# Two transformer-like blocks on one core: the last round of the second FFN up-projection as block products, and its weight sums made on the side

## The reference

```python
x = x + gate_m * (jnp.concatenate([attn, rec], axis=-1) @ w_out[l])    # output projection, 1024 x 1024
h = rms_norm_2(x, ffn_norm_g[l]) * (1 + scale_f) + shift_f
u, v = jnp.split(h @ w_up[l], 2, axis=-1)                              # 1024 x (2816 + 2816)
u = causal_depthwise_conv(u, conv_w[l], conv_b[l])                     # 3 taps
x = x + gate_f * ((jax.nn.silu(u) * v) @ w_down[l])                    # 2816 x 1024
return rms_norm_2(x, final_norm_g)
```

## Time and profile before

| | |
|---|---|
| median of 3 runs | 1339.14 us (1339.03 to 1342.26) |
| the profiled execution: its own time | 1340.83 us |
| the profiled execution: its span, first to last instruction | 1339.0 us |
| PE busy | 1325.6 us (99%), 8520 matmuls |
| PEld busy | 1143.1 us (85%) |
| DVE / ACT / POOL busy | 874.9 (65%) / 643.3 (48%) / 682.4 (51%) us |
| mean granted TensorE clock | 0.997 |
| HBM read / written | 185.55 / 33.55 MB |

### The profile page before, as it was taken

One profiled execution on the slowest core, in us unless ns is written; L12 is line 12 of the kernel. 1 busy time (PEld: TensorE's weight loads), 2 busy tenths in 40 slices (PEclk: granted clock), 3 DMA queues, 4 the chain that ended last, 5 costly groups with the idle time before them and its releaser, 6 DMA issues.

```text
span 1339.0 us, 22719 instructions
## 1 busy us (share of the span) xinstructions
PE 1325.6 (99%) x8520; PEld 1143.1 (85%) x8520; DVE 874.9 (65%) x1711; ACT 643.3 (48%) x1146; POOL 682.4 (51%) x378
## 2 busy tenths in 40 slices
PE   8999999999999999999999999999999999999998
PEld 7878888888998888888889986778998999998887
DVE  5898976455778676767897878823479655541222
ACT  7336566464255444444222535585364666642222
POOL 7577444326354444444553489743355555554441
PEclk9999999999999999999999999999999999999999
DMA  6985696865525444444673241265335457452221
GB/s 216 226 266 203 193 154 110 121 101 170 176 80 177 153 141 141 141 147 142 204 232 124 64 126 34 64 119 87 95 134 166 134 172 213 143 208 91 87 87 63
DMA packets 251210, 191.00 MB, mean 143 GB/s; under 512 B 23001, under 2 KB 245443, under 8 KB 250608
## 3 DMA queue, kind: packets, MB, share of 16 engines
q1 hardware_dynamic: 216896, 159.79, 39.1%
q0 software_dynamic: 33024, 29.61, 12.1%
q10 hardware_dynamic: 1200, 0.36, 0.1%
HBM read 185.55 MB, written 33.55 MB: 164 GB/s over the span
## 4 chain that ended last, share of the span: by engine, by line
PE 95%; DVE 3%; ACT 1%; DMA 1%; issue 0%; SPq 0%; DVEq 0%; ACTq 0%
PE ps L2744 28%; PE ps L2745 28%; PE ps L2746 28%; PE ps L2938 2%; PE ps L2994 1%; PE ps L3023 1%; DVE qd L2394 1%; DVE hf L2402 1%; PE ps L3226 1%; DMA x_in<-in_x 1%; PE ps L3270 0%; PE ps L3255 0%; PE ps L3199 0%; DVE hs L2437 0%; PE ps L3292 0%
## 5 line engine op out<-in xcount | busy, mean ns | idle before, releaser
L973 POOL TENSOR_TENSOR w_lo<-raw,w_hi 128x1024 fp32r<-128x1024 f32 (+2 forms) x196 | 457.1, 2337 | 514.6 <-ACT w_hi L1108 381.2
L2744 PE MATMUL ps<-h_hi,w_hi 128*128 128x512 f32 (+1 forms) x1280 | 459.3, 359 | 0.0
L2745 PE MATMUL ps<-h_lo,w_hi 128*128 128x512 f32 (+1 forms) x1280 | 454.9, 355 | 0.0
L2746 PE MATMUL ps<-h_hi,w_lo 128*128 128x512 f32 (+1 forms) x1280 | 454.8, 355 | 0.0
L2744 PEld LDWEIGHTS ps<-h_hi,w_hi 128*128 128x128 f32 x1280 | 243.0, 190 | 37.7 <-issue 4.9
L2746 PEld LDWEIGHTS ps<-h_hi,w_lo 128*128 128x128 f32 x1280 | 242.7, 190 | 34.4
L2745 PEld LDWEIGHTS ps<-h_lo,w_hi 128*128 128x128 f32 x1280 | 243.1, 190 | 31.9
L1108 ACT ACTIVATE w_hi<-raw 128x1024 fp32r<-128x1024 f32 (+2 forms) x152 | 150.1, 990 | 240.6 <-PE ps L2746 215.3
L2744 PE MATMUL ps<-g_hi,w_hi 128*128 128x512 f32 (+1 forms) x394 | 145.0, 368 | 0.0
L2745 PE MATMUL ps<-g_lo,w_hi 128*128 128x512 f32 (+1 forms) x394 | 144.5, 367 | 0.0
L2746 PE MATMUL ps<-g_hi,w_lo 128*128 128x512 f32 (+1 forms) x394 | 144.5, 367 | 0.0
(11 more groups left out here) (413 smaller groups left out, 2163.3 us busy)
## 6 DMA issues: line engine op xcount, KB each, us to landing
ada<-in_ada_w SPq DMA_DIRECT2D x48, 512.0 KB, 3.8
raw<-in_ffn_w_up SPq DMA_DIRECT2D x22, 1024.0 KB, 4.9
raw<-in_w_in SPq DMA_DIRECT2D x21, 1024.0 KB, 5.3
kept_sums<-in_w_up POOLq DMA_DIRECT2D x12, 1792.0 KB, 11.9
raw<-in_w_up SPq DMA_DIRECT2D x8, 1024.0 KB, 5.0
kept_sums<-kept_sums POOLq DMA_DIRECT2D x4, 1792.0 KB, 15.8
raw<-in_ffn_w_down SPq DMA_DIRECT2D x8, 896.0 KB, 6.1
sums<-kept_sums SPq DMA_DIRECT2D x28, 256.0 KB, 5.5
```

Source lines behind the costliest of these rows:

```text
L973: pool.tensor_tensor(w_lo[w_slot(slot)][:, 0:nk, :], part[:, :, slot % 2 * P:(slot % 2 + 1) * P], w_hi[w_slot(slot)][:, 0:nk, :].bitcast(F ...
L2744: pe.matmul(out_ap, w, x, start=first, stop=False, **kw)
L2745: pe.matmul(out_ap, w, xl, start=False, stop=False, **kw)
L2746: return pe.matmul(out_ap, wl, x, start=False, stop=last, **kw)
```

## The change

- `R1` becomes 11: the rounds 3 to 10 are block products, in 16 pairs instead of 14, and the plain round 10 goes. Its four entries in the orders of ACT, DVE and PE go with it.
- The sums of weights for round 10 are made apart from those of the seven rounds before. POOL issues four copies of 512 KB, both kinds at once (`begin_sum(n, None)`), after `lo(S_OUT2 + 3)`, once all eight earlier adding transfers have landed. It then issues two adding transfers of 512 KB after `lo(S_OUT2 + 5)`, once the four copies have landed, a third after `lo(S_OUT2 + 7)`, once these two have landed, and the fourth after `lo(S_UP2 + 1)`, once the third has. SP waits for all 16 adding transfers and copies in question before it loads the first pair.
- The sets of PSUM banks are swapped: even pairs take banks 0 to 3, and the last plain round (tiles 164 to 167) takes banks 4 to 7. The two matmuls of L3323 and L3324 go.
- The last pair's first product on DVE (`gated_up(10, 0)`) waits for both results of the pair, because the low part of the fourth activation sum lies where its output goes.
- `kept_sums` has 8 rounds to a row instead of 7, so the adding transfers from one sum to the other walk rows of 7 x 128 instead of one flat run.

```diff
-R0, R1 = 3, FT // 2 - 1
+R0, R1 = 3, FT // 2
...
-            bank[s] = s % 4 + (4 if AFTER <= s < S_DOWN2 else 0)
+            bank[s] = s % 4 + (4 if PAIR_TILE - 4 <= s < PAIR_TILE else 0)
...
         def kept_blocks(kind, t, kh):
 
+            w = a["w_up_2"][0][kh * 4 * P:(kh + 1) * 4 * P, :]
+            if kind is None:
+                c = up_columns(R1 - 1, 0) + t * P
+                return w.rearrange("k (c f) -> k c f", c=2)[:, :, c:c + P]
             c = up_columns(R0, kind)
-            w = a["w_up_2"][0][kh * 4 * P:(kh + 1) * 4 * P, c:c + (R1 - R0) * 256]
-            return w.rearrange("k (r t n) -> k r t n", t=2, n=P)[:, :, t, :]
-
-        PAIR_SET = lambda p: 4 * ((p + 1) % 2)
+            return w[:, c:c + (R1 - 1 - R0) * 256].rearrange("k (r t n) -> k r t n", t=2, n=P)[:, :, t, :]
+
+        def kept_at(n, kind):
+
+            if kind is None:
+                return kept_sums[n - 1].rearrange("c k r n -> k c r n")[:, :, R1 - 1 - R0, :]
+            return kept_sums[n - 1][kind, :, 0:R1 - 1 - R0, :]
+
+        PAIR_SET = lambda p: 4 * (p % 2)
...
-            sp.wait_ge(sums_kept, SUMS_BEGUN + 16 * 8)
+            sp.wait_ge(sums_kept, SUMS_BEGUN + 16 * 16)
...
             def add_to_sum(n, kind):
...
+                pool.wait_ge(sums_kept, SUMS_BEGUN + 16 * ADDED_BEFORE[n, kind])
+                more = {1: lambda: kept_blocks(kind, 1, 1), 2: lambda: kept_at(1, kind),
+                        3: lambda: kept_blocks(kind, 1, 0), 4: lambda: kept_at(2, kind)}[n]()
+                pool.dma_start(kept_at(n, kind), more, accum_op=ALU.add, max_dma_last_dim=4 * P).then_inc(sums_kept, 16)
...
+            ADDED_BEFORE = {(1, 0): 0, (1, 1): 0, (3, 0): 0, (3, 1): 0, (2, 0): 4, (2, 1): 4, (4, 0): 6, (4, 1): 6,
+                            (1, None): 12, (3, None): 12, (2, None): 14, (4, None): 15}
...
+                         S_OUT2 + 5: [(1, None), (3, None)], S_OUT2 + 7: [(2, None)], S_UP2 + 1: [(4, None)]}
 
             def kept(s):
-                if s in ADD_STEPS:
-                    add_to_sum(*ADD_STEPS[s])
+                if s == S_OUT2 + 3:
+                    pool.wait_ge(sums_kept, SUMS_BEGUN + 16 * 8)
+                    for n in (1, 2, 3, 4):
+                        begin_sum(n, None)
+                for step in ADD_STEPS.get(s, ()):
+                    add_to_sum(*step)
...
-            for j in range(4):
-                hi(S_DOWN2 + j)
-                if j < 2:
-                    first_tap(R1, j)
-                else:
-                    silu(R1, j - 2)
-            for t in range(2):
-                g_high(R1, t)
...
-                dve.wait_ge(tile_done, up_tile(r, 1, t) + 1)
+                dve.wait_ge(tile_done, up_tile(r, 1, t) + (1 if r + 1 < R1 else 2 - t))
...
-            for t in range(2):
-                taps2(R1, t)
-            for t in range(2):
-                gated_up(R1, t)
-            for t in range(2):
-                g_low(R1, t)
...
-                if s == PAIR_TILE - 1:
-                    pe.wait_ge(lo_done, lows(s))
-                    pe.matmul(ps[5][:, 0:HALF], w_hi[s % 4][:, 0, :], h_hi[:, 0, 0:HALF], start=True, stop=True)
-                    pe.matmul(ps[6][:, HALF:T], w_hi[s % 4][:, 0, :], h_hi[:, 0, 0:HALF], start=True, stop=True)
                 tile(s, h_hi, h_lo)
...
-            pe.wait_ge(freed["dve"], after_pair(NPAIR - 1))
```

More of the change, by code:

```diff
@@ L337, in build @@
         t_at = [(ada_at, ada_at + 4096), (x_at, x_at + 4096), (x_at + 8192, x_at + 12288),
-                (G0 + 4 * T * 2 * R1, G0 + 4 * T * (FT + 2 * R1))]
+                (G0 + 4 * T * (FT - 2), G0 + 4 * T * (2 * FT - 2))]
         t_hi = [sb(f"t{n + 1}_hi", [P, 4, HALF], F32R, at=t_at[n][0])[:, :, :] for n in range(4)]
@@ L821, in hgrn_pool @@
                 lo(s)
+                kept(s)
         def add_late_squares(pool, b):
@@ L983, in begin_sum @@
                 t, kh = {1: (1, 0), 2: (0, 0), 3: (0, 0), 4: (0, 1)}[n]
-                pool.dma_start(kept_sums[n - 1][kind], kept_blocks(kind, t, kh)).then_inc(sums_kept, 16)
+                pool.dma_start(kept_at(n, kind), kept_blocks(kind, t, kh)).then_inc(sums_kept, 16)
             def add_to_sum(n, kind):
-                if n == 1:
-                    pool.wait_ge(sums_kept, SUMS_BEGUN)
-                elif n in (2, 4):
-                    pool.wait_ge(sums_kept, SUMS_BEGUN + 16 * (4 if n == 2 else 6))
@@ L992, in add_to_sum @@
-                more = {1: lambda: kept_blocks(kind, 1, 1), 2: lambda: kept_sums[0][kind],
-                        3: lambda: kept_blocks(kind, 1, 0), 4: lambda: kept_sums[1][kind]}[n]()
-                pool.dma_start(kept_sums[n - 1][kind], more, accum_op=ALU.add, max_dma_last_dim=4 * P).then_inc(sums_kept, 16)
-            SUM_STEPS = dict(zip([*range(S_V, S_MERGE), S_MERGE + 3, S_MERGE + 4], itertools.product((1, 2, 3, 4), range(2))))
-            ADD_STEPS = dict(zip([S_MERGE + n for n in (6, 8, 11, 13, 15)] + [S_ATTN + 2, S_OUT2 - 2, S_OUT2],
-                                 itertools.product((1, 3, 2, 4), range(2))))
@@ L1000, in kept @@
-            def kept(s):
-                if s in ADD_STEPS:
-                    add_to_sum(*ADD_STEPS[s])
+                pool.wait_ge(sums_kept, SUMS_BEGUN + 16 * ADDED_BEFORE[n, kind])
+                more = {1: lambda: kept_blocks(kind, 1, 1), 2: lambda: kept_at(1, kind),
+                        3: lambda: kept_blocks(kind, 1, 0), 4: lambda: kept_at(2, kind)}[n]()
+                pool.dma_start(kept_at(n, kind), more, accum_op=ALU.add, max_dma_last_dim=4 * P).then_inc(sums_kept, 16)
+            SUM_STEPS = {s: [step] for s, step in zip([*range(S_V, S_MERGE), S_MERGE + 3, S_MERGE + 4],
+                                                      itertools.product((1, 2, 3, 4), range(2)))}
@@ new lines, in _ @@
+            ADDED_BEFORE = {(1, 0): 0, (1, 1): 0, (3, 0): 0, (3, 1): 0, (2, 0): 4, (2, 1): 4, (4, 0): 6, (4, 1): 6,
+                            (1, None): 12, (3, None): 12, (2, None): 14, (4, None): 15}
+            ADD_STEPS = {S_MERGE + 6: [(1, 0)], S_MERGE + 8: [(1, 1)], S_MERGE + 11: [(3, 0)], S_MERGE + 13: [(3, 1)],
+                         S_MERGE + 15: [(2, 0)], S_ATTN + 2: [(2, 1)], S_OUT2 - 2: [(4, 0)], S_OUT2: [(4, 1)],
+                         S_OUT2 + 5: [(1, None), (3, None)], S_OUT2 + 7: [(2, None)], S_UP2 + 1: [(4, None)]}
@@ L1059, in _ @@
                     pool.wait_ge(low_or_gated, LOW_BEHIND[s])
-                if s in SUM_STEPS:
-                    begin_sum(*SUM_STEPS[s])
+                for step in SUM_STEPS.get(s, ()):
+                    begin_sum(*step)
                 kept(s)
```

## The result

| | before | after |
|---|---|---|
| median, us | 1341.76 (1339.03 to 1346.47, 20 runs) | 1347.39 (1342.62 to 1356.26, 20 runs) |
| profiled span and own time, us | 1339.0 and 1340.83 | 1343.7 and 1345.4 |
| granted clock | 0.997 | 0.997 |

The ratio is 1.0045, 95% interval 1.0033 to 1.0057: the kernel is slower by 4.4 to 7.6 us where 1.9 us less was forecast. The forecast in microseconds leaned on three runs of before at 1339.14; over 20 runs that kernel is at 1341.76, so 2.6 us of the distance to the forecast is the base and the rest the change.

The account below looks back on a forecast made before the run. PE, with 95% of the chain that ended last, was taken to bound the kernel. Savings of 1.63 and 0.23 us, 1.86 together with nothing added, took the median from 1339.14 to 1337.3 us, range 1336.5 to 1341.

Parts of the forecast that it names:

- PE's sum: Round 10 as two pairs instead of plain saves PE 1.63 us, the two dropped matmuls of L3323 and L3324 0.23 us.
- The border to the down-projection: Down-projection directly after pair 15: its first tile, banks and residual load come in time; cost taken as nothing.
- The copies: Four small copies on POOL behind tile 151: 1.02 us each to issue, landed at 949 to 956, taken as 952.5.
- Two adding issues later, at 955.2, tile 154 is subtracted ... hidden, with 3 us left: POOL in the output projection: after the copies and two adding issues, tile 154 ready at 957.6, PE wants it at 960.66.
- the late copies: Rival: the small copies land late for tile 154 in the output projection; result 1338.5 to 1343 us, chance 0.10.
- the slow chain: Rival: landing does not shrink with size, POOL waits for the third transfer, PE stands 11.7 us; 1349 to 1351, chance 0.07.
- The fourth issue: Last small adding issue on POOL, ahead of tile 158 and the squares: 1.09 us from a line over rows, cost nothing.
- the prediction's own cover of 1.42 us: Slack around the fourth issue before PE takes the squares' sum: 0.84 us ahead of tile 158 plus 0.58 us.
- the rival: The fourth issue is as long as a large one, PE stands 1.2 to 2.2 us: 1338.5 to 1339.5, chance 0.14.
- small issues over 1.4 us: Stated sign of being wrong: any of the small issues on POOL takes over 1.4 us.
- a wait of POOL for the third transfer past 977: Stated sign of being wrong: POOL waits longer than 977 for the third small adding transfer to land.
- The strided rows of the large transfers: Two large adding transfers in the output projection's lead may take 3.61 instead of 2.64 us to issue; cost taken as nothing.

Follow-up runs that it names:

- pairs only: Changed kernel without small transfers, flat rows for the large ones, last two pairs taking the sums of the pairs before them: 1339.69 us, ratio 0.999 to before.
- the three comparisons of times: Strided against flat rows: with adding transfers moved alike (ratios 0.0023 apart), in the changed kernel (0.0019), and in the kernel before (0.0010).
- ten flat profiles: Profiles of the kernels whose large transfers keep flat rows, the kernel before among them; in the others round 10's sums have a tensor of their own, `kept_last`.
- four strided ones: Profiles with eight-round rows: the changed kernel, it with adding transfers moved (1342.13 us), with only the fourth moved (1344.78), and the kernel before with that layout (1343.41).
- A copy behind the adding transfer: Changed kernel with flat rows and the fourth small copy issued behind the first small adding transfer: 1343.32 us, one run.
- Halved adding transfers: Changed kernel with flat rows and the first two small adding transfers issued in two halves each: 1345.25 us, one run.
- Placed: Changed kernel with flat rows, first small adding transfer alone, second and third sum's two products later, fourth behind the squares: 1339.2 us, ratio 0.9974 to before.
- The fourth copy later: Changed kernel with flat rows, fourth small copy behind the third adding transfer, fourth adding transfer behind the squares: 1340.13 us, ratio 0.9984 to before.

## Why the prediction was wrong

- **PE's sum** (1.63 + 0.23 us): right, at 1.62 + 0.26. The block products are 161.28 us long where 161.3 were forecast; pairs only is 1.3 us shorter in span and 0.1% in time. One reading beside it was off, without a term that hung on it: 120 and 227 ns are 13 to 14 ns above the columns' own time, not 11 to 13.
- **The border to the down-projection**, taken at nothing: right. The matmuls keep their spacing across it, and no wait of PE lies there.
- **The copies**, landed by 952.5: nearly, they landed by 953.92. They cost 5.15 / 4 = 1.29 us each, not 1.02, and the first adding issue behind them stands at 954.22.
- **"Two adding issues later, at 955.2, tile 154 is subtracted ... hidden, with 3 us left": the step that failed.** The second issue found no room and stood 5.67 us. The low part ended at 965.98 instead of 957.6, and PE stood 2.9 us. No rival had this: the late copies and the slow chain both looked at landings that the program waits for, not at a stand inside an issue. Yet it was in a row shown there: the third large copy has "[4.04 <-issue]" ahead of it, read then for its 2.34 us alone.
- **The fourth issue**, taken at 1.09 us by a line over rows: measured 2.32 to 2.35 us for 1,024 rows between sums, 1.83 to 1.89 us out of the weights. PE stood 0.9 us, as the prediction's own cover of 1.42 us gives with an issue of 2.35; the rival had priced 1.2 to 2.2 us for it, with a chance of 0.14. The line went through copies and was scaled down for adding transfers; by the rows an adding issue of 1,024 rows costs about half to nine tenths of one of 3,584 (3.61 and 2.64). Of the prediction's own signs of being wrong this one came, small issues over 1.4 us; a wait of POOL for the third transfer past 977 did not.
- **The strided rows of the large transfers**, taken at nothing with 0.97 us as the most: they take 4.5 us to issue, but that is hidden. What costs is earlier, in the large copies, which were not looked at: 2.1 us of stands at PE by the profiles of the changed kernel, and 1.3 to 3.1 us by the three comparisons of times, none of them clear of noise by itself.
- **The clock**: the two stands did not lower it. In the three microseconds of the first one, the clock column reads 1.00 (windows of after: us, busy PE to POOL, clock, DMA share, GB/s):

```profile
963.00:966.00 3.00, 0.12 (x2) 0.00 (x0) 2.84 (x2) 0.42 (x1) 3.00 (x3) 1.00 0.50 52
```

The sum over the profiled executions closes: -1.62 for the block products, -0.26 for the two matmuls of L3323 and L3324 and what lies with them, +4.28 for the two stands and what they shift, +2.31 ahead of the output projection, +4.71 in all; measured 1343.7 - 1339.0 = 4.7. The medians say 5.6 us (4.4 to 7.6), so about 1 us may lie outside what the one profile shows. The +2.31 is the least sure piece: the output projection begins between 931.9 and 935.1 us in the ten flat profiles and between 935.2 and 939.9 in the four strided ones, so the layout's part of it is known to a microsecond or two only.

The Trainium skill, "Collectives: The Full Stack" (section "The bandwidth ceiling: the fold count and why AG ≠ RS ≠ AR"), says that a reducing transfer writes two read descriptors for each chunk and a copy one. The runs agree with its ratio, in another use: with an added row at two places and a copied row at one, each of the small transfers' stands comes at a count of 8 units, and whatever came at 7.5 or under went out at once.

When places come free can be read from the same profiles, though no kernel was made to test it: not one by one as transfers land, but all at once. A stand ended only when every transfer issued before it had landed. In "A copy behind the adding transfer" the first adding transfer had landed at 958.1, yet the stand lasted until the copy behind it had, at 959.48 (chain that ended last; the first row is that copy, from its issue to its landing):

```profile
952.15 7.33 DMA kept_last<-in_w_up
959.48 0.26 issue
959.74 1.82 POOL kept_last L1004
```

In "Halved adding transfers" the three halves landed at 955.8, 957.7 and 960.2, and the fourth went at 960.44. In before the first large copy landed at 79.4 us and the second at 85.8; the third, with POOL idle since 82.3, went at 86.37. So a simple count fits: every issue adds its units, landed or not; one that would bring the count to 8 waits until all before it have landed, and the count starts again with it. From the first large copy on this fits every one of POOL's issues to the sums in all 14 profiles, with 3.5 units for a large copy and 7 for a large adding transfer. It also says why "Placed" (6 + 2 at 961.13) and "The fourth copy later" (7 + 2 at 962.35) pass 8 without such a stand: by then everything before had landed, at 960.7 and 961.9. What stays open is what sets the size of the room. The kernel's `dynamic_dma_scratch_size=8192` was the same in all runs.

## What to carry to other kernels

An idle time of GpSimd ahead of a DMA issue, ended by "issue" or by a transfer for which the program does not wait there, is a price of its own. Before a burst of transfers is put in front of work that another engine waits for, count the rows that GpSimd has issued, the landed ones too and an adding transfer's twice, from the last issue that would have filled the room. Spread the burst, or leave one copy out of it; here one copy less ahead, with the fourth adding transfer behind the squares, turned a ratio of 1.0026 into 0.9984. And a change of layout can be paid by every transfer that touches the tensor, also by those 800 microseconds earlier that the diff seems to leave alone.

## What the runs showed of the hardware

- For GpSimd's transfers from HBM to HBM 7.5 units of 1,024 rows fitted (an added row counted twice, landed rows counted still) and 8 did not. An issue that did not fit stood for 5.6 to 6.3 us with small transfers and 4.0 to 9.4 us with large ones, and went 0.3 to 0.5 us after the last of all earlier ones had landed.
- An issue of 1,024 rows of 512 bytes takes 1.27 to 1.37 us as a copy, 1.82 to 1.89 us as an adding transfer out of the weights, and 2.31 to 2.35 us as one between sums, also where those lie contiguously, if no other issue stands directly ahead. A quarter of an adding one took 0.87 us, a half 1.01 us.
- Strided rows raised the large adding issues from 3.6 and 2.64 us to 4.5 or 4.6 us in the changed kernel, and to 4.1 to 4.3 us in the kernel before.
- In the changed kernel small transfers of 512 KB landed in 6.4 to 9.2 us and large ones of 1792 KB in 9.9 to 21.2 us: less than in proportion.
- Two stands of PE, of 2.9 and 0.9 us, left the granted clock at 1.00.
